# Two sets of weight sums at other places in VectorE's order, in the seven-product part of a feed-forward layer

## The chip, the cores and the metric

The kernel runs on one core of one Trainium2 chip. The metric is the device time of one execution in microseconds (us); the time of a kernel is the median of its runs.

## The reference

A trunk of two layers (`DEPTH = 2`) on 256 tokens of width 1024, in float32. Each layer is a feed-forward block, a mixing block (a state-space group beside a gated group), and a second feed-forward block; a final RMSNorm ends it. The change lies in the second feed-forward block:

```python
def swiglu(h, w_in, w_out):
    gu = h @ w_in
    g, u = gu[..., :D_FF], gu[..., D_FF:]
    return (jax.nn.silu(g) * u) @ w_out

for l in range(DEPTH):
    x = x + 0.5 * swiglu(rmsnorm(x, norm_ffn1[l]), ffn1_w_in[l], ffn1_w_out[l])
    ...
    x = x + 0.5 * swiglu(rmsnorm(x, norm_ffn2[l]), ffn2_w_in[l], ffn2_w_out[l])
```

`D_FF` is 2816, which is 22 tiles of 128 (`FT`) or 11 blocks of 256 (`UB`).

## The kernel before

Every product is made from numbers split in two parts: `hi`, a copy in the matmul's own format (float32r), and `lo`, the rest. A product is then three matmuls (`three`, L501 to L503: hi x hi, hi x lo, lo x hi). ScalarE makes `hi` (`ACTIVATE` with Copy), VectorE makes `lo` (a subtraction).

**Halves and slots.** Weights come in through three `raw` buffers of 1 MB, issued by SyncE, and are split into a ring of four halves (`RING = 4`), `w_hi` and `w_lo`. A half is 128 rows x 1024. The halves of a feed-forward block are numbered by h from its start: h = 0 to 43 are the up projection (4 per block of 256 hidden columns, 11 blocks), h = 44 to 65 the 22 rows tiles of the down projection. The same number orders ScalarE's and VectorE's work by hand: each walks over h, and tables say which further work stands at which h. TensorE consumes a half and counts `half_done`; ScalarE may split half n only after half n - 4 is consumed.

**Seven products.** In ffn2, the second feed-forward block, 12 of the 22 row tiles of the down projection are taken in pairs, as six slots (`SEVEN = (3, ..., 8)`, h = 50 to 61), numbered i = 0 to 5 below. A slot's 2x2 product of blocks is done with seven block products in place of eight (`seven_rows`). For this, sums of the hidden values (`sums_a`, then `hs_hi`, `hs_lo`) and sums of the weights are needed. The weights are loaded a second time into an `area` (two in `sums_b`, two more over the memory of `x_hi` and `x_lo`, which is free when the up projection has ended). `sums_make` builds four sums in an area with four VectorE operations (L1334, L1336, L1338, L1340), each of which waits for the one before. `sums_split` makes `s_hi` on ScalarE (L994) and `s_lo` on VectorE (L1348). There are two `s_hi`/`s_lo` buffers; ScalarE writes one only after TensorE has finished the slot two before (`seven_done`). The plain weights of such a slot are split as one wide operation of 1536 columns at its even h (L1007 on ScalarE, L1319 on VectorE).

**TensorE's waits.** At the first slot, and at each after it, TensorE waits for all the hidden values and for the wide split; it then does three products (nine matmuls) with plain weights, waits for the slot's `s_lo`, and does four more (twelve matmuls):

```python
pe.wait_ge(hlo_done, UB * f + UB)
pe.wait_ge(salo_done, l * N7 + i + 1)
...
pe.wait_ge(lo_done, half(l, h) + 2)
...
pe.wait_ge(slo_done, m + 1)
```

**VectorE's order.** `ffn` walks over h, and inside one h the order is fixed:

```python
split(l, UPS[j] + h)
if j:
    sums_split(l, h)
    sums_make(l, h)
if j and h - 1 in HIDDEN_AT and HIDDEN_AT.index(h - 1) in SEVEN:
    sums_lo(l, HIDDEN_AT.index(h - 1))
if h in HIDDEN_AT:
    hidden_lo(l, j, HIDDEN_AT.index(h))
```

`HIDDEN_AT` places the hidden blocks; its last three entries, for blocks 8, 9 and 10, are 4 UB + 5, 4 UB + 6 and 4 UB + 7, with 4 UB = 44. `hidden_lo` (L1445) writes `h_lo` and counts `hlo_done`. `SUMS_AT`, `SPLIT_AT` and `LOAD_AT` place the sums, the splits of the sums and the loads of the areas, one entry for each slot i.

Of the kernel before, what the change touches and what calls it, by code (L numbers as in the profile page):

```python
# [19 lines left out]
UB = FF // 256  # L20
# [53 lines left out]

AREA = (0, 1, 0, 1, 2, 3)
LOAD_AT = (26, 28, 36, 38, 4 * UB + 8, 4 * UB + 10)
SUMS_AT = (25, 29, 36, 41, 4 * UB + 9, 4 * UB + 12)
SPLIT_AT = (28, 31, 4 * UB + 11, 4 * UB + 13, 4 * UB + 15, 4 * UB + 17)
FOLD_AT = 4 * UB + 2 * SEVEN[-1] + 5

# [58 lines left out]
def build(nc, a, out):  # L139
    stack = ExitStack()  # L140
    with stack:
# [1164 lines left out]
        def _(dve):  # L1306
# [20 lines left out]
            def sums_make(l, h):  # L1327

                for i in range(N7):
                    if SUMS_AT[i] == h:  # L1330
                        m = l * N7 + i
# [598 lines left out]
```

## Time and profile before

| | |
|---|---|
| median of 3 runs | 907.9 us (907.88 to 907.93) |
| the profiled execution | 907.8 us |
| its span, first to last instruction | 906.1 us |
| TensorE matmul busy | 897.4 us (99%) |
| VectorE busy | 620.3 us (68%) |
| ScalarE busy | 507.4 us (56%) |
| GpSimd busy | 371.8 us (41%) |
| mean DMA rate | 193 GB/s |

Engines are named PE (TensorE matmul), PEld (TensorE weight load), DVE (VectorE), ACT (ScalarE), POOL (GpSimd) and SP (SyncE). A line of the timeline has the start in us, the length in us, the engine, the line of the kernel, the operation, out<-in, and the count of merged instructions. In brackets stands how long the engine was idle before it and what released it. Matmuls are pipelined: the length of one reaches over the start of the next, so their pace is read from their starts. Layer 0's ffn2 has its down projection from about 391 us, layer 1's from about 837 us.

### The profile page before, as it was taken

The page shows a single profiled execution, that of the slowest core. Times are in us where ns is not written, and L with a number is a line of the kernel's source. Part 1 is how long each engine was busy: PE and PEld are TensorE (multiplying, and loading weights), DVE is VectorE, ACT ScalarE, POOL GpSimd, SP SyncE. Part 2 cuts the span into 40 slices and gives each one's busy share as a digit, 9 for nine tenths or more (in the row PEclk, how much of TensorE's full clock was granted, in tenths as well). Part 3 has the DMA queues.
Part 4 walks back from the last instruction along what each step waited for, and adds up shares of the span by engine and source line. Part 5 has one row for each costly group of instructions (what it writes and reads, how often), then busy time and mean ns, then how long its engine had stood idle before and what let it go on. Part 6 is the DMA issues. An engine that isn't in the chain of part 4 may idle for free.

```text
span 906.1 us, 12882 instructions
## 1 busy us (share of the span) xinstructions
PE 897.4 (99%) x4935; PEld 743.1 (82%) x4935; DVE 620.3 (68%) x729; ACT 507.4 (56%) x741; POOL 371.8 (41%) x574
## 2 busy tenths in 40 slices
PE   9999999999999999999999999999999999999997
PEld 7888888888878888887888888888888888888886
DVE  5555665458976578868965656653888855789597
ACT  6544454458766456646464445445677654656474
POOL 3488999894510000000055889988734100000000
PEclk9999999999999999999999999999999999999999
DMA  9786555544256677684559665555344476785751
GB/s 281 196 271 188 186 184 180 175 160 142 94 194 200 196 251 230 229 283 159 186 175 246 186 188 186 186 186 186 120 160 143 139 221 196 263 270 188 267 175 46
DMA packets 138381, 174.60 MB, mean 193 GB/s; under 512 B 18760, under 2 KB 110032, under 8 KB 138320
## 3 DMA queue, kind: packets, MB, share of 16 engines
q1 hardware_dynamic: 138032, 173.24, 59.7%
q8 instruction: 39, 0.64, 0.3%
q10 hardware_dynamic: 288, 0.53, 0.2%
q14 instruction: 22, 0.18, 0.1%
HBM read 172.70 MB, written 1.05 MB: 192 GB/s over the span
## 4 chain that ended last, share of the span: by engine, by line
PE 95%; DVE 3%; issue 1%; DMA 1%; ACT 1%; SPq 0%; ACTq 0%; DVEq 0%
PE bank L501 29%; PE bank L503 29%; PE bank L502 29%; PE bank L606 2%; DVE w_lo L1319 1%; PE bank L511 1%; PE bank L833 1%; DVE s_lo L1348 1%; DMA raw<-in_ffn_w_in 1%; PE bank L861 0%; PE bank L851 0%; PE bank L874 0%; PE bank L716 0%; ACT w_hi L1007 0%; PE bank L937 0%
## 5 line engine op out<-in xcount | busy, mean ns | idle before, releaser
L1324 DVE TENSOR_TENSOR w_lo<-raw,w_hi 128x1024 fp32r<-128x1024 f32 x278 | 351.0, 1271 | 214.4 <-ACT w_hi L1016 214.2
L1016 ACT ACTIVATE w_hi<-raw 128x1024 fp32r<-128x1024 f32 x278 | 292.7, 1061 | 242.0 <-PE bank L503 223.2
L501 PE MATMUL bank<-w_hi,x_hi 128*128 128x512 f32 x856 | 336.5, 393 | 0.0
L503 PE MATMUL bank<-w_hi,x_lo 128*128 128x512 f32 x856 | 333.5, 390 | 0.0
L502 PE MATMUL bank<-w_lo,x_hi 128*128 128x512 f32 x856 | 333.2, 389 | 0.0
L501 PEld LDWEIGHTS bank<-w_hi,x_hi 128*128 128x128 f32 x856 | 160.7, 188 | 35.2 <-issue 2.5
L503 PEld LDWEIGHTS bank<-w_hi,x_lo 128*128 128x128 f32 x856 | 160.7, 188 | 33.7
L502 PEld LDWEIGHTS bank<-w_lo,x_hi 128*128 128x128 f32 x856 | 160.8, 188 | 32.3
L1664 POOL TENSOR_TENSOR rstd_c<-ms_c,neg_half 128x2 f32<-128x2 f32 (+1 forms) x7 | 7.7, 1106 | 394.9 <-DVE ms_c L1367 394.9
L501 PE MATMUL bank<-w_hi,h_hi 128*128 128x512 f32 (+1 forms) x283 | 111.0, 392 | 0.0
L503 PE MATMUL bank<-w_hi,h_lo 128*128 128x512 f32 (+1 forms) x283 | 109.7, 387 | 0.0
L502 PE MATMUL bank<-w_lo,h_hi 128*128 128x512 f32 (+1 forms) x283 | 109.6, 387 | 0.0
L1079 ACT ACTIVATE sil<-bank,rstd_c 128x256 f32<-128x256 f32 x88 | 36.8, 470 | 53.2 <-PE bank L503 53.1
L501 PEld LDWEIGHTS bank<-w_hi,h_hi 128*128 128x128 f32 x283 | 53.1, 188 | 11.4 <-DVE h_lo L1445 0.6
L503 PEld LDWEIGHTS bank<-w_hi,h_lo 128*128 128x128 f32 x283 | 53.1, 188 | 11.0
L502 PEld LDWEIGHTS bank<-w_lo,h_hi 128*128 128x128 f32 x283 | 53.2, 188 | 10.4
L1655 POOL TENSOR_TENSOR sc<-sc 128x16 f32<-128x16 f32 (+1 forms) x154 | 55.2, 358 | 12.3
L1428 DVE SCALAR_TENSOR_TENSOR hid<-bank,rstd_c,sil 128x256 f32<-128x256 f32 x88 | 38.5, 479 | 24.4 <-ACT sil L1079 24.4
L1655 POOL TENSOR_TENSOR pt<-sc,bp 128x256 f32<-128x256 f32 x56 | 52.6, 940 | 4.4
L1658 POOL TENSOR_SCALAR sc<-sc 128x16 f32<-128x16 f32 (+1 forms) x90 | 38.7, 430 | 7.7
L1655 POOL TENSOR_TENSOR bp<-pt 128x256 f32<-128x256 f32 x32 | 36.3, 1133 | 2.5
L1319 DVE TENSOR_TENSOR w_lo<-raw,w_hi 128x1536 fp32r<-128x1536 f32 x12 | 21.0, 1753 | 12.9 <-ACT w_hi L1007 12.9
(231 smaller groups left out, 886.9 us busy)
## 6 DMA issues: line engine op xcount, KB each, us to landing
raw<-in_ffn_w_in SPq DMA_DIRECT2D x172, 512.0 KB
raw<-in_ffn_w_out SPq DMA_DIRECT2D x32, 1024.0 KB
raw<-in_mix_w_in SPq DMA_DIRECT2D x12, 1024.0 KB
raw<-in_mix_w_out SPq DMA_DIRECT2D x8, 1024.0 KB
sums_b<-in_ffn_w_out SPq DMA_DIRECT2D x16, 512.0 KB, 6.9
raw<-in_ffn_w_out SPq DMA_DIRECT2D x12, 512.0 KB
area<-in_ffn_w_out SPq DMA_DIRECT2D x8, 512.0 KB, 6.4
raw<-in_ffn_w_out SPq DMA_DIRECT2D x12, 256.0 KB
```

What stands on the lines that cost most here:

```text
L501: mm(o, hi_a, hi_b, start=first, stop=False)
L502: mm(o, hi_a, lo_b, start=False, stop=False)
L503: return mm(o, lo_a, hi_b, start=False, stop=last)
L511: ins = nc.tensor.transpose(turned(pair, j)[:, h * P:h * P + P], x[:, h, k * P:k * P + P], ident[:, :])
L606: ins = nc.tensor.transpose(hidden_bank(l, j, b)[:, c:c + P], hid[:, b % 4, h, ft * P:ft * P + P], ident[:, :])
L1016: A(w_hi[:, n % RING, :], raw[:, s, (n % 2) * 1024:(n % 2) * 1024 + 1024], ACT.Copy).then_inc(hi_done, 1)
L1079: A(sil[:, b % 2, t, :], bank[2 * pair + t][:, 0:256], ACT.Silu, scale=rstd_c[:, t:t + 1]).then_inc(sil_done, 1)
L1319: TT(w_lo[:, n % RING:n % RING + 2, :].rearrange("p s m -> p (s m)")[:, 0:1536], raw[:, s, 0:1536], w_hi[:, n % RING:n % RING + 2, :].rear ...
L1324: TT(w_lo[:, n % RING, :], raw[:, s, (n % 2) * 1024:(n % 2) * 1024 + 1024], w_hi[:, n % RING, :].bitcast(F32), ALU.subtract).then_inc(lo_d ...
L1428: STT(hid[:, b % 4, t, :], bank[2 * pair + t][:, 256:512], rstd_c[:, t:t + 1], sil[:, b % 2, t, :], ALU.mult, ALU.mult).then_inc(hid_done, 1)
L1655: link(nc.gpsimd.tensor_tensor(o, x0, x1, op))
L1658: link(nc.gpsimd.tensor_scalar(o, x0, s1, s2, op0, op1))
```

## The change

Two entries of the table `SUMS_AT` change. The four sums of slot i=4 stand at h = 51 in place of 53, and those of slot i=5 at h = 58 in place of 56. Loads, splits and everything on the other engines keep their places.

```diff
 AREA = (0, 1, 0, 1, 2, 3)
 LOAD_AT = (26, 28, 36, 38, 4 * UB + 8, 4 * UB + 10)
-SUMS_AT = (25, 29, 36, 41, 4 * UB + 9, 4 * UB + 12)
+SUMS_AT = (25, 29, 36, 41, 4 * UB + 7, 4 * UB + 14)
 SPLIT_AT = (28, 31, 4 * UB + 11, 4 * UB + 13, 4 * UB + 15, 4 * UB + 17)
```

## Rows read from the trace of the kernel before

**Rows 1.** The page: span, busy time by engine, chain that ended last.
```profile
span 906.1 us, 12882 instructions
...
PE 897.4 (99%) x4935; PEld 743.1 (82%) x4935; DVE 620.3 (68%) x729; ACT 507.4 (56%) x741; POOL 371.8 (41%) x574
...
PE 95%; DVE 3%; issue 1%; DMA 1%; ACT 1%; SPq 0%; ACTq 0%; DVEq 0%
```

**Rows 2.** The chain in order of time, layer 0: start, length, what.
```profile
413.64 1.50 ACT w_hi L1007
...
428.01 2.29 DVE s_lo L1348
```

**Rows 3.** TensorE's timeline, layer 0, slots i=0 and i=3.
```profile
413.13 0.39 PE L503 MATMUL bank<-w_hi,h_lo 128*128 128x512 f32 x1
413.40 0.50 PE L501 MATMUL bank<-w_hi,h_hi 128*128 128x512 f32 x1
...
418.30 0.39 PE L501 MATMUL bank<-w_hi,h_hi 128*128 128x512 f32 x1
...
429.64 0.39 PE L503 MATMUL bank<-w_hi,h_lo 128*128 128x512 f32 x1
430.35 0.50 PE L501 MATMUL bank<-s_hi,hs_hi 128*128 128x512 f32 x1 [0.32 <-DVE s_lo L1348]
...
433.20 0.39 PE L501 MATMUL bank<-w_hi,h_hi 128*128 128x512 f32 x1
```

**Rows 4.** TensorE's timeline, layer 1, the same two places.
```profile
859.71 0.50 PE L501 MATMUL bank<-w_hi,h_hi 128*128 128x512 f32 x1
...
876.65 0.50 PE L501 MATMUL bank<-s_hi,hs_hi 128*128 128x512 f32 x1 [0.33 <-DVE s_lo L1348]
```

**Rows 5.** VectorE's timeline, layer 0, from h = 50 to h = 54.
```profile
409.79 1.76 DVE L1319 TENSOR_TENSOR w_lo<-raw,w_hi 128x1536 fp32r<-128x1536 f32 x1 [4.58 <-ACT w_hi L1007]
411.47 0.68 DVE L1452 TENSOR_TENSOR hs_lo<-sc,hs_hi_last 128x512 fp32r<-128x512 f32 x1
412.07 1.28 DVE L1445 TENSOR_TENSOR h_lo<-bank,h_hi 128x512 fp32r<-128x512 f32 x2
415.23 1.76 DVE L1319 TENSOR_TENSOR w_lo<-raw,w_hi 128x1536 fp32r<-128x1536 f32 x1 [1.88 <-ACT w_hi L1007]
416.90 0.69 DVE L1334 TENSOR_TENSOR area<-area 128x512 f32<-128x512 f32 x1
...
419.69 1.75 DVE L1319 TENSOR_TENSOR w_lo<-raw,w_hi 128x1536 fp32r<-128x1536 f32 x1
```

**Rows 6.** TensorE's weight loads, timeline, ahead of slot i=0.
```profile
413.40 0.19 PEld L501 LDWEIGHTS bank<-w_hi,h_hi 128*128 128x128 f32 x1 [0.31 <-DVE h_lo L1445]
```

**Rows 7.** Windows: us, PE, PEld, DVE, ACT, POOL busy, clock, DMA share, GB/s.
```profile
404.00:408.00 4.00, 4.00 (x19) 3.28 (x19) 1.18 (x3) 0.00 (x0) 0.00 (x0) 1.00 0.97 339
408.00:412.00 4.00, 4.00 (x20) 3.30 (x18) 2.21 (x2) 2.98 (x4) 0.00 (x0) 1.00 0.06 23
```

**Rows 8.** VectorE's timeline, layer 0, from h = 57 to h = 59.
```profile
428.01 2.28 DVE L1348 TENSOR_TENSOR s_lo<-sums_b,s_hi 128x2048 fp32r<-128x2048 f32 x1
430.21 1.75 DVE L1319 TENSOR_TENSOR w_lo<-raw,w_hi 128x1536 fp32r<-128x1536 f32 x1
431.88 2.28 DVE L1348 TENSOR_TENSOR s_lo<-area,s_hi 128x2048 fp32r<-128x2048 f32 x1
```

**Rows 9.** ScalarE's timeline, layer 0, `s_hi` of slots i=2 and i=3.
```profile
418.56 1.92 ACT L994 ACTIVATE s_hi<-sums_b 128x2048 fp32r<-128x2048 f32 x1 [1.21 <-PE bank L503]
...
423.32 1.93 ACT L994 ACTIVATE s_hi<-sums_b 128x2048 fp32r<-128x2048 f32 x1 [1.20 <-PE bank L503]
```

**Rows 10.** Windows at the end of the span, columns as in rows 7.
```profile
900.00:901.00 1.00, 0.17 (x2) 0.00 (x0) 0.80 (x3) 0.84 (x4) 0.83 (x1) 1.00 0.74 168
...
903.00:903.50 0.50, 0.00 (x0) 0.00 (x0) 0.00 (x0) 0.00 (x0) 0.00 (x0) 0.95 0.62 131
903.50:904.00 0.50, 0.00 (x0) 0.00 (x0) 0.00 (x0) 0.00 (x0) 0.00 (x0) 0.50 0.86 180
```

## The prediction

> **What bounds the kernel now.** I read the page first. TensorE is busy for 897.4 of 906.1 us and makes 95% of the chain that ended last; VectorE has 3% of it [rows 1]. So the time is TensorE's queue plus its few gaps, and a change in VectorE's order counts only where it opens or closes a gap on TensorE. Next I read the chain in order of time around the edited step, the second half of ffn2. From 413.64 to 430.30 us in layer 0 it leaves TensorE and runs through ScalarE and VectorE up to a split of sums, `s_lo` L1348 [rows 2]. VectorE is the limit of that stretch, and the gap that it leaves on TensorE is all that a better order can win.
>
> I took the size of that gap from TensorE's timeline. Matmuls of a seven-product step start every 0.227 us: from 413.40 to 418.30 are 21 of them and a start-up (below), and without a wait a step is 21 x 0.227 = 4.76 us. Step i=3 shows the gap: from the matmul at 429.64 to the first of step i=4 at 433.20 are 13 starts, which would be 2.95 us; it took 3.56. The gap is 0.61 us per layer, released by `s_lo` L1348 [rows 3]. Layer 1 has the same wait at 876.65 [rows 4]. Two gaps of 0.61 are 1.2 us, 0.13% of the time, the most that the change can win. Two runs of this kernel can be told apart from about 0.2% (1.8 us) on, so that gain alone would not show.
>
> **Where the moved work lands.** A slot's sums are four VectorE operations of 128x512, L1334 to L1340. In the kernel before, those of slot i=4 start at 416.90 and the next operation starts at 419.69: 2.79 us [rows 5]. No operation is added or removed, and no DMA, wait or other queue moves; only VectorE's order changes. What counts is what stands behind the 2.79 us in each new place.
>
> *Slot i=4, from h = 53 to h = 51.* In `ffn` on VectorE the body of h runs `sums_make` before `hidden_lo`. HIDDEN_AT has 4 UB + 6 = 50 for block 9 and 4 UB + 7 = 51 for block 10. So the order in the stretch from 409.79 was: wide split of h = 50, `hs_lo`, `h_lo` of block 9, `h_lo` of block 10 [rows 5]. Now the four sums stand between the two `h_lo`. The two took 1.28 us together from 412.07, and one alone takes 0.68, as `hs_lo` of the same size does, so the second started at 412.67 and ended at 413.35.
>
> Who waits for that second `h_lo`? TensorE does: ahead of the first seven-product step it waits for `hlo_done` of all 11 blocks (UB * f + UB). The last ordinary matmul started at 413.13 and the next could start at 413.36. It started at 413.40, 0.05 us after `h_lo` ended [rows 3], and the weight load in front of it has an idle time of 0.31 us with DVE `h_lo` L1445 as its releaser [rows 6]. There is no slack to speak of: VectorE arrives 0.01 us before TensorE is ready to go on. That is the observation on which the forecast rests.
>
> The new times: sums from 412.67 to 415.46, `h_lo` of block 10 to 416.14, TensorE starts at 416.19 in place of 413.40. **The new stall costs 2.79 us per layer.** Nothing moves it earlier. The wide split of h = 50 starts at 409.79 after 4.58 us in which VectorE waited for ScalarE [rows 5], and from there VectorE works without a pause to the `h_lo`. The sums' input is there: the DMA engines were still at 97% until 408 us and at 6% from 408 to 412, so the transfers of the two areas, issued ahead of that, have landed [rows 7]. No cost for a wait on the transfer, then; if it were late, VectorE would wait at the sums and all of that would be added.
>
> Can TensorE make the 2.79 us up later? No: it has no idle time to give but the gap of 0.61 us, and every later step is queued behind.
>
> *Slot i=5, from h = 56 to h = 58.* These sums stood ahead of `s_lo` of slot i=3, which TensorE was waiting for at 430.35 [rows 3, 8]. Now they stand behind it. In addition TensorE is 2.79 us later. ScalarE's `s_hi` of slot 3 follows TensorE's step i=1 and moves with it from 423.32 to 426.11, ending at 428.04 [rows 9]. VectorE is free by then: `s_hi` of slot 2, which ran from 418.56 for 1.92 us [rows 9], moves by 2.79 too and ends at 423.27; `s_lo` takes 2.20 and a wide split 1.67 after it [rows 8], which makes 427.2. So `s_lo` of slot 3 runs from 428.08 to 430.36, and TensorE needs it at 429.87 + 2.79 = 432.66. **The old gap goes: -0.61 us per layer.**
>
> What is late next? Behind it stand the wide split of h = 58, the sums of slot 5 and `s_lo` of slot 4. From one start to the next, `s_lo` takes 2.20 us and a wide split 1.67 [rows 8]. So the split starts at 430.28, the sums at 431.95, `s_lo` of slot 4 at 434.74, and it ends at 437.02. TensorE starts step i=4 at 433.20 - 0.61 + 2.79 = 435.38 and needs `s_lo` after nine matmuls, at 437.42. The margin is 0.40 us: thin, but it holds by these rows. `s_lo` of slot 5 ends at 434.74 + 2.20 + 1.67 + 2.28 = 440.89 and is needed at 442.18; a margin of 1.3 us. After that come plain splits, where VectorE is ahead.
>
> **The sum.** Per layer +2.79 - 0.61 = +2.18 us, in two layers +4.36 us. Layer 1 runs the same way: from TensorE's start at step i=0 to its wait in step i=3 are 876.65 - 859.71 = 16.94 us there [rows 4] and 430.35 - 413.40 = 16.95 us in layer 0 [rows 3]. The profiled execution took 907.8 us (span 906.1 and 1.7 around it), and the median of the runs is 907.9. Both give the same shift: 907.9 + 4.4 = 912.3 us, +0.48%.
>
> **A page against a row.** TensorE will stand still for about 2.7 us in each layer, longer than anywhere in the span now. At the end of the span its last matmul starts before 900.2; the granted clock is still 1.00 in the stretch to 903, 0.95 in the one to 903.5 and 0.50 (the lower level, 1.2 GHz) from then on [rows 10]. So it fell some 3.3 us after the work ended, and 2.7 us of idle time is shorter than that. The Trainium skill ("TensorE: Matmul & The Clock Gate", "Why this matters for your kernels") warns of idle gaps between bursts of matmuls, because the engine goes back to its lower level after them. By the row the sum stays 912.3; by the rule, if this gap counted, it would be the 915.6 of the second rival.
>
> **Rivals.**
> 1. *The new wait isn't exposed; only the old gap closes.* If TensorE had slack at the first seven-product step, the sums of slot 4 would hide under its rows and the 1.2 us would be won: 906.7 us, not slower. For it: VectorE was idle for 4.58 us just before, so on a mean there is room. Against it: that room lies ahead of the wide split, not between the two `h_lo`, and TensorE's weight load already waits for `h_lo` [rows 6]. It would take more than 2 us of slack for this side to win; the rows show 0.01. Chance 0.07.
> 2. *The clock falls in the stall.* If TensorE came back at 1.2 GHz and stayed there for as long as it takes to fall, 3.3 us, half of that would be lost: 1.65 us per layer, 3.3 in all, 915.6 us. For it: the instant of the fall is known here only once. Against it: 2.7 is under 3.3, and in the 0.61 us gap the clock didn't move. Chance 0.05.
> 3. *The margin of 0.40 us at step i=4 doesn't hold.* The gap then comes back there: up to the 0.61 us of the old one, 1.2 us in all, 913.5 us. Speaking for it: VectorE works without a pause from 428.08 on, and a delay of each of its four steps by 0.1 us uses the margin up. Against: the same operations took the same time to within 0.01 us in all of this stretch. Chance 0.08.
>
> **How the numbers follow.** My forecast has 0.80: 912.3 us, its own range 911.7 to 913.0 (a tenth of a microsecond on each of the eight edges, and the start-up after a longer wait, of which the trace has only short examples). The range is 911.3 to 913.9: the forecast and rival 3, with a little on both sides for a stall a few tenths smaller or larger than the sum says. Rivals 1 and 2 lie outside. Slower by over 0.2%: forecast, rivals 2 and 3, 0.93. Rival 1 is -0.13%, so most of its 0.07 falls within 0.2%: same 0.05, faster 0.02.
>
> **What the profile after would show.** In TensorE's timeline an idle time of about 2.7 us ahead of the first matmul of step i=0 near 416.2 us, released by DVE `h_lo` L1445, and the same in layer 1 near 864.7. In VectorE's timeline four `area` operations between two single `h_lo`. No wait for `s_lo` L1348 in the middle of step i=3. Granted clock 1.00 right after the stall. `s_lo` of slot 4 ends within half a microsecond of TensorE's need. The prediction is wrong if TensorE's start at step i=0 doesn't move, if the chain keeps `s_lo` of slot 3, or if the clock reads less than 1.00 after 416 us.

## The result and the profile after

The changed kernel takes 915.45 us (median of 6 runs, 914.48 to 915.94) against 908.03 us before: a ratio of 1.008, 95% interval 1.0067 to 1.0093. It is 7.4 us slower. The sign and the place are as forecast, but the time lies 1.5 us above the range and the loss is 1.7 times the 4.4 us of the sum. It comes out where the second rival put it, at 915.6 us.

The profiled execution of the changed kernel took 915.6 us with a span of 913.9. TensorE's timeline around the first seven-product step of layer 0, which answers to [rows 3]:

```profile
413.33 0.39 PE L503 MATMUL bank<-w_hi,h_lo 128*128 128x512 f32 x1
416.39 0.50 PE L501 MATMUL bank<-w_hi,h_hi 128*128 128x512 f32 x1 [2.67 <-DVE h_lo L1445]
416.73 0.39 PE L502 MATMUL bank<-w_lo,h_hi 128*128 128x512 f32 x1
416.96 0.50 PE L503 MATMUL bank<-w_hi,h_lo 128*128 128x512 f32 x1
417.25 0.63 PE L501 MATMUL bank<-w_hi,hs_hi 128*128 128x512 f32 x1
417.68 0.63 PE L502 MATMUL bank<-w_lo,hs_hi 128*128 128x512 f32 x1
...
420.24 0.52 PE L502 MATMUL bank<-s_lo,hs_hi 128*128 128x512 f32 x1
420.60 0.39 PE L503 MATMUL bank<-s_hi,hs_lo 128*128 128x512 f32 x1
...
422.91 0.39 PE L501 MATMUL bank<-w_hi,h_hi 128*128 128x512 f32 x1
```

Two things are to be seen. TensorE stands idle for 2.67 us, released by `h_lo`. And after the restart the next starts come after 0.34, 0.23 and 0.29 us, then every 0.43 us in place of 0.227, until about 420.5 us. The windows of the same stretch tell why (columns as in [rows 7]; the clock is the third figure from the right):

```profile
415.00:416.00 1.00, 0.00 (x0) 0.00 (x0) 0.97 (x3) 0.33 (x1) 0.00 (x0) 1.00 0.19 72
416.00:417.00 1.00, 0.61 (x3) 0.53 (x4) 1.00 (x2) 0.00 (x0) 0.00 (x0) 1.00 0.00 0
417.00:418.00 1.00, 1.00 (x4) 0.80 (x3) 1.00 (x1) 0.00 (x0) 0.00 (x0) 0.55 0.00 0
418.00:419.00 1.00, 1.00 (x4) 0.72 (x4) 0.00 (x0) 0.00 (x0) 0.00 (x0) 0.50 0.00 0
419.00:420.00 1.00, 1.00 (x4) 0.82 (x3) 0.00 (x0) 0.00 (x0) 0.00 (x0) 0.50 0.97 207
420.00:422.00 2.00, 2.00 (x10) 1.61 (x9) 0.28 (x1) 1.49 (x1) 0.00 (x0) 0.87 0.76 289
422.00:424.00 2.00, 2.00 (x10) 1.68 (x9) 1.48 (x1) 0.83 (x1) 0.00 (x0) 1.00 0.00 1
```

The granted clock is 1.00 through the whole idle time. It falls to 0.50 at about 417.1 us, when TensorE has been at work again for 0.7 us, and comes back at about 420.5. Layer 1 does the same:

```profile
863.44 0.39 PE L503 MATMUL bank<-w_hi,h_lo 128*128 128x512 f32 x1
866.49 0.50 PE L501 MATMUL bank<-w_hi,h_hi 128*128 128x512 f32 x1 [2.66 <-DVE h_lo L1445]
...
873.02 0.39 PE L501 MATMUL bank<-w_hi,h_hi 128*128 128x512 f32 x1
```

VectorE's timeline shows the moved sums between the two `h_lo`, as answer to [rows 5], and slots 3 and 4 behind, as answer to [rows 8]:

```profile
410.00 1.76 DVE L1319 TENSOR_TENSOR w_lo<-raw,w_hi 128x1536 fp32r<-128x1536 f32 x1 [4.58 <-ACT w_hi L1007]
411.67 0.68 DVE L1452 TENSOR_TENSOR hs_lo<-sc,hs_hi_last 128x512 fp32r<-128x512 f32 x1
412.27 0.68 DVE L1445 TENSOR_TENSOR h_lo<-bank,h_hi 128x512 fp32r<-128x512 f32 x1
412.88 0.68 DVE L1334 TENSOR_TENSOR area<-area 128x512 f32<-128x512 f32 x1
...
415.65 0.68 DVE L1445 TENSOR_TENSOR h_lo<-bank,h_hi 128x512 fp32r<-128x512 f32 x1
416.25 1.75 DVE L1319 TENSOR_TENSOR w_lo<-raw,w_hi 128x1536 fp32r<-128x1536 f32 x1
...
429.88 2.29 DVE L1348 TENSOR_TENSOR s_lo<-sums_b,s_hi 128x2048 fp32r<-128x2048 f32 x1 [0.80 <-ACT s_hi L994]
...
436.54 2.28 DVE L1348 TENSOR_TENSOR s_lo<-area,s_hi 128x2048 fp32r<-128x2048 f32 x1
```

From start to start the sums still take 415.65 - 412.88 = 2.77 us. The old gap at step i=3 is gone from the list of TensorE's waits in the changed kernel.

**The loss by rows.** In layer 0 the step starts 416.39 - 413.33 = 3.06 us after the matmul before it, and 0.27 us after it in [rows 3]: 2.79 us lost, the term of the sum. The step then takes 422.91 - 416.39 = 6.52 us, against 4.90 in [rows 3]: 1.62 us more. Layer 1 has 3.05 us ahead of the step, of which 0.28 were there before (859.71 - 859.43), and 6.53 us for the step. With the old gap gone, a layer loses 2.79 + 1.62 - 0.61 = 3.80 us, the two 7.6; the spans differ by 7.8, and 0.2 of this was there before the first edited stretch (413.33 against 413.13).

### The profile page after: what moved, and what is told of

Read it like the earlier page. It is cut to its first block, busy times and chain, and to the rows that moved or that the text cites. A ratio compares the mean times of both kernels' runs of the same rounds, so it can differ in the third digit from the quotient of the medians.

```text
span 913.9 us, 12882 instructions
## 1 busy us (share of the span) xinstructions
PE 901.0 (99%) x4935; PEld 746.5 (82%) x4935; DVE 620.7 (68%) x729; ACT 507.4 (56%) x741; POOL 370.7 (41%) x574
## 4 chain that ended last, share of the span: by engine, by line
PE 97%; DVE 1%; ACT 0%; issue 0%; POOL 0%; ACTq 0%; POOLq 0%; DVEq 0%
PE bank L501 30%; PE bank L503 29%; PE bank L502 29%; PE bank L606 2%; PE bank L511 1%; PE bank L833 1%; PE bank L861 0%; PE bank L851 0%; PE bank L966 0%; PE bank L874 0%; DVE w_lo L1319 0%; PE bank L716 0%; ACT w_hi L1007 0%; PE bank L937 0%; PE bank L539 0%; DVE h_lo L1445 0%
## 5 line engine op out<-in xcount | busy, mean ns | idle before, releaser
L1655 POOL TENSOR_TENSOR sc<-sc 128x16 f32<-128x16 f32 (+1 forms) x154 | 59.1, 384 | 12.3
L1658 POOL TENSOR_SCALAR sc<-sc 128x16 f32<-128x16 f32 (+1 forms) x90 | 34.2, 380 | 7.7
```

The lines of the kernel that those rows point to most:

```text
L1655: link(nc.gpsimd.tensor_tensor(o, x0, x1, op))
L1658: link(nc.gpsimd.tensor_scalar(o, x0, s1, s2, op0, op1))
```

## Experiments

The medians are those of 5 or 11 runs. The times of the kernel before beside them were 908.12 us (slot 5 alone, slot 4 alone, no sum ahead, 24 transposes) and 908.26 us (12 transposes and one, two and three sums ahead).

### Slot 5 alone

```diff
-SUMS_AT = (25, 29, 36, 41, 4 * UB + 9, 4 * UB + 12)
+SUMS_AT = (25, 29, 36, 41, 4 * UB + 9, 4 * UB + 14)
```

> Only slot i=5 moves (h = 56 to 58); slot i=4 stays at h = 53. Theory: this half closes the old gap of 0.61 us per layer at step i=3 and opens none, since s_lo of slot 4 would end near 434.2 us and TensorE needs it near 434.6. Expected 906.7 us (907.9 - 1.2), clock 1.00 throughout. Rival (the move of slot 5 itself costs something at step i=4): 908 us or more, with a wait for s_lo L1348 one step later.

Measured: 906.84 us, ratio 0.9983 (0.9974 to 0.9992). This half gains 1.3 us, the 1.2 of the sum. TensorE's timeline at step i=3 runs at full pace over the place of the old gap:

```profile
430.20 0.39 PE L503 MATMUL bank<-w_hi,h_lo 128*128 128x512 f32 x1
430.43 0.39 PE L501 MATMUL bank<-s_hi,hs_hi 128*128 128x512 f32 x1
430.66 0.39 PE L502 MATMUL bank<-s_lo,hs_hi 128*128 128x512 f32 x1
```

The start behind the wait comes 0.23 us after the one ahead of it, where [rows 3] have 0.71. The rival falls: no wait for `s_lo` appears one step later.

### Slot 4 alone

```diff
-SUMS_AT = (25, 29, 36, 41, 4 * UB + 9, 4 * UB + 12)
+SUMS_AT = (25, 29, 36, 41, 4 * UB + 7, 4 * UB + 12)
```

> Only slot i=4 moves (h = 53 to 51); slot i=5 stays at h = 56. Theory: the whole loss comes from this half, the stall of 2.7 us before the first seven-product step and the fall of the clock behind it, and the delay of TensorE also covers the old wait for s_lo of slot 3. Expected 915.4 us, like the changed kernel, clock 0.995. Rival (the 0.61 us per layer were won back by the move of slot 5): 916.6 us, with a wait for s_lo L1348 in step i=3.

Measured: 915.62 us, ratio 1.0078 (1.0065 to 1.0091), the time of the changed kernel. The row of TensorE's waits that names slot work (total us, times, longest us):

```profile
PE bank L501 <- DVE h_lo L1445: 5.3, 2, 2.7
```

That is two waits of 2.7 us for `h_lo`, and none for `s_lo`. So the whole loss is slot 4's, and in its company slot 5's move gains nothing: TensorE is so late that the old wait vanishes by itself.

The trace of this kernel also shows when a fall may come. TensorE's timeline and the windows, layer 0:

```profile
413.62 0.39 PE L503 MATMUL bank<-w_hi,h_lo 128*128 128x512 f32 x1
416.67 0.79 PE L501 MATMUL bank<-w_hi,h_hi 128*128 128x512 f32 x1 [2.66 <-DVE h_lo L1445]
```

```profile
416.00:416.25 0.25, 0.00 (x0) 0.00 (x0) 0.25 (x2) 0.00 (x0) 0.00 (x0) 1.00 0.00 0
416.25:416.50 0.25, 0.00 (x0) 0.00 (x0) 0.25 (x1) 0.00 (x0) 0.00 (x0) 0.58 0.00 0
```

The idle time begins at 414.01 us and the clock falls at about 416.3, some 2.3 us later and 0.4 us before TensorE starts again. In layer 1 it falls at about 866.85 us, 3.0 us after the idle time began. The time from the start of the idle time to the fall isn't a constant. Part of the fall of layer 0 costs nothing, since it lies in the idle time: the step takes 423.00 - 416.67 = 6.33 us there, 0.19 less than in the changed kernel.

### The sums of slot 4 behind the last `h_lo`

The changed kernel, with its new table, but at h = 51 the four sums stand at the end of the body. `sums_make` is written as a loop for this, with the same four operations in the same order; its third argument says which of them it does:

```diff
-                        sums_make(l, h)
+                        sums_make(l, h, range(0) if h == HIDDEN_AT[-1] else range(4))
...
                     if h in HIDDEN_AT:
                         hidden_lo(l, j, HIDDEN_AT.index(h))
+                    if j and h == HIDDEN_AT[-1]:
+                        sums_make(l, h, range(0, 4))
```

> The changed kernel with the four sums of slot i=4 at the end of the body of h = 51, behind h_lo of block 10 in place of ahead of it. Theory (TensorE loses only because the sums stand ahead of that h_lo; behind it VectorE has an idle 1.9 us before the next wide split, and 0.5 us of margin at step i=1): no stall, clock 1.00, old gap gone: 906.7 us. Rival (sums this early cost something whatever stands behind them, through the wide split of h = 52 or the ring): 909 us or more.

Measured: 906.86 us, ratio 0.9986 (0.9977 to 0.9995). One operation of 0.6 us changes sides with the four sums, and 8.6 us come back. VectorE's timeline (a loop makes the four sums one line here):

```profile
412.38 1.28 DVE L1444 TENSOR_TENSOR h_lo<-bank,h_hi 128x512 fp32r<-128x512 f32 x2
413.58 2.86 DVE L1339 TENSOR_TENSOR area<-area 128x512 f32<-128x512 f32 x4
416.36 3.42 DVE L1319 TENSOR_TENSOR w_lo<-raw,w_hi 128x1536 fp32r<-128x1536 f32 x2
```

The sums fill the 1.88 us in which VectorE waited for ScalarE before [rows 5]; the wide splits behind are later for it, but TensorE's list of waits has none for `w_lo`. The sums may be that early; they may only not stand ahead of that `h_lo`.

### TensorE kept at work during its wait, for 2.8 us and for 1.5 us

The changed kernel, with 24 or 12 transposes of the identity in each layer that add nothing to the result (the next product that is written to their bank starts it anew):

```diff
                             i = SEVEN.index(k // 2)
+                            if i == 0:
+                                for _ in range(24):
+                                    nc.tensor.transpose(bank[2 * c0 + 1][:, 0:P], ident[:, :], ident[:, :])
                             pe.wait_ge(hlo_done, UB * f + UB)
```

> The changed kernel, and TensorE does 24 transposes of the identity into an unused bank (about 0.109 us each, 2.6 us) in each layer ahead of its wait for h_lo, so that it is delayed as before but not idle. Theory A (the excess over the predicted 912.3 us is the clock that falls after the idle time): clock 1.00, 912.3 us. Theory B (the excess is something else in the longer stall, such as later weights or a slower restart): 915.4 us, clock figures notwithstanding.

> The changed kernel with 12 transposes (1.3 us) ahead of TensorE's wait for h_lo: the same delay of 2.79 us, but only 1.4 us of it idle. Theory A (it is the length of idle time that makes the clock fall, not the delay): clock 1.00 and 913.0 us, as with 24 transposes. Theory B (the delay matters, or any stall here): 915.4 us.

Measured: 913.00 us with 24 (ratio 1.0053, 1.004 to 1.0065) and 912.59 us with 12 (1.0047, 1.0034 to 1.006). TensorE's timeline with 24:

```profile
414.26 2.78 PE L788 MATMUL bank<-ident 128*128 128x128 f32 x24
417.08 0.50 PE L501 MATMUL bank<-w_hi,h_hi 128*128 128x512 f32 x1
417.42 0.39 PE L502 MATMUL bank<-w_lo,h_hi 128*128 128x512 f32 x1
417.65 0.40 PE L503 MATMUL bank<-w_hi,h_lo 128*128 128x512 f32 x1
417.89 0.39 PE L501 MATMUL bank<-w_hi,hs_hi 128*128 128x512 f32 x1
```

and with 12:

```profile
414.48 1.47 PE L788 MATMUL bank<-ident 128*128 128x128 f32 x12
417.30 0.50 PE L501 MATMUL bank<-w_hi,h_hi 128*128 128x512 f32 x1 [1.35 <-DVE h_lo L1448]
417.64 0.40 PE L502 MATMUL bank<-w_lo,h_hi 128*128 128x512 f32 x1
```

The windows of the same stretch, with 24 and with 12:

```profile
412.00:422.00 10.00, 9.96 (x57) 8.44 (x56) 7.46 (x10) 3.06 (x3) 0.00 (x0) 1.00 0.46 149
```

```profile
417.30:422.00 4.70, 4.70 (x20) 3.86 (x21) 2.23 (x2) 1.49 (x1) 0.00 (x0) 1.00 0.43 130
```

The step starts as late as in the changed kernel, but the matmuls behind it keep their pace of 0.23 us and the clock stays at 1.00. More work on TensorE makes the kernel 2.5 to 2.9 us faster than the changed one. Against their own runs of before they cost 4.9 and 4.3 us, where the sum without a clock term says 4.4. So the delay is priced rightly, and the excess goes with the idle time and not with the delay; an effect of late weights would have stayed. That it is the clock, and not another slowness after a long idle time, is read from the changed kernel: the starts come every 0.43 us just where its windows read 0.50.

### One, two and three of the four sums ahead of the last `h_lo`

As the third experiment, with `range(n)` ahead and `range(n, 4)` behind.

> One of the four sums stands ahead of the last h_lo. Delay 0.6 to 0.7 us, idle time about 0.5 us, no more than the old gap at step i=3, behind which the clock stayed: 907.9 us by both theories (the new gap is as large as the old one), clock 1.00.

> Two of the four sums stand ahead of the last h_lo. Delay 1.33 us, idle time about 1.2 us. Theory A: no fall, 907.9 + 2 x (1.33 - 0.61) = 909.3 us. Theory B: 912.3 us.

> Three of the four sums of slot i=4 stand ahead of the last h_lo at h = 51, the fourth behind it. TensorE's delay is 3 x 0.72 less the overlap, 2.06 us; its idle time about 1.9 us. Without a fall of the clock 907.9 + 2 x (2.06 - 0.61) = 910.8 us; with a fall in both layers (1.5 us each, as the changed kernel shows) 913.8 us. Theory A (the fall needs an idle time near that of the changed kernel, 2.7 us): 910.8. Theory B (any stall at this place makes it fall): 913.8.

| sums ahead of `h_lo` | TensorE idle before step i=0, us | expected without a fall, us | measured, us (lowest to highest) | ratio, interval |
|---|---|---|---|---|
| 0 | none | 906.7 | 906.86 (906.24 to 907.29) | 0.9986 (0.9977 to 0.9995) |
| 1 | 0.5 | 907.9 | 908.16 (907.66 to 909.04) | 0.9999 (0.999 to 1.0008) |
| 2 | 1.2 | 909.3 | 909.50 (909.17 to 909.96) | 1.0014 (1.0005 to 1.0023) |
| 3 | 1.9 | 910.8 | 911.72 (910.6 to 912.7) | 1.0037 (1.0024 to 1.0049) |
| 4 (the changed kernel) | 2.7 | 912.3 | 915.45 (914.48 to 915.94) | 1.008 (1.0067 to 1.0093) |

The expected times start from 907.9 us. Up to two sums the price follows the delay alone. With three, both theories are half right: the two layers of the profiled execution go different ways after the same idle time. TensorE's timeline of that kernel, layer 0 and then layer 1, and a window of layer 1:

```profile
415.28 0.50 PE L501 MATMUL bank<-w_hi,h_hi 128*128 128x512 f32 x1 [1.94 <-DVE h_lo L1444]
...
420.20 0.39 PE L501 MATMUL bank<-w_hi,h_hi 128*128 128x512 f32 x1
...
862.99 0.50 PE L501 MATMUL bank<-w_hi,h_hi 128*128 128x512 f32 x1 [1.94 <-DVE h_lo L1444]
...
864.26 0.53 PE L503 MATMUL bank<-w_hi,hs_lo 128*128 128x512 f32 x1
864.58 0.63 PE L501 MATMUL bank<-w_hi,h_hi 128*128 128x512 f32 x1
...
869.54 0.39 PE L501 MATMUL bank<-w_hi,h_hi 128*128 128x512 f32 x1
```

```profile
864.00:866.00 2.00, 2.00 (x7) 1.55 (x6) 1.21 (x1) 0.00 (x0) 0.00 (x0) 0.59 0.00 0
```

Step i=0 takes 4.92 us in layer 0 and 6.55 in layer 1, where the clock fell about 1.4 us after the restart. One fall costs 1.63 us, read from one execution with everything else alike. Whether it comes after 1.9 us of idle time is not the same from one place to the next.

The other runs have no profile, but each has a mean granted clock. It is 0.995 in the two profiled executions with two falls, 0.997 in the one with one fall, and 0.998 to 1.000 in every run of the kernels whose profile shows no fall before the end of the span. Read by this scale, which is an inference, the five runs with three sums ahead had no fall in two (910.60 and 911.23 us; clock 0.998 and 0.999) and one in the other three (911.72, 912.15 and 912.70 us; 0.996, 0.997 and 0.997; the 0.996 fits least well). And 2.7 us of idle time doesn't bring a fall each time either: of the 11 runs of the changed kernel and of slot 4 alone, three read 0.997 (914.48, 914.22 and 914.39 us) and eight 0.995 (915.01 to 916.06 us).

## Why the prediction failed, by its steps

- *What bounds the kernel; a gain of at most 1.2 us.* Right. Slot 5 alone gave 1.3.
- *Slot 4 lands ahead of the `h_lo` that TensorE waits for, 2.79 us per layer.* Right to 0.02 us in both layers (2.79 and 2.77), and shown by moving the sums behind that `h_lo`, which takes all of it away.
- *Slot 5's move closes the old gap, -0.61 us per layer.* Right as a size (slot 5 alone), wrong as a cause inside the whole change: with slot 4 alone the gap is gone too, and the time is the same. Once TensorE is 2.8 us later, `s_lo` of slot 3 is in time in either order. The sum counts the term rightly, as a property of the delay.
- *The margin of 0.40 us at step i=4.* Right: `s_lo` of slot 4 ended at 438.82 us, and the matmul behind TensorE's wait for it started at 439.23, 0.41 us later. Both are 1.8 us later than forecast: ScalarE and VectorE followed TensorE's delay. The third rival didn't happen.
- *"2.7 us of idle time is shorter than that."* **This is the step that failed.** I read from [rows 10] that the clock fell 3.3 us after the last matmul of the span, took this as the idle time which a fall needs, and so put the clock at nothing in the sum. It cost 3.2 us, 1.62 in each layer. The row was one example with nothing behind it. In the changed kernel the idle time was 2.7 us and the fall came 3.4 us (layer 0) and 3.8 us (layer 1) after it began, when the matmuls were running again; with slot 4 alone, layer 0, it came after 2.3 us. At the end of the span, too, the 3.3 us of [rows 10] are only one of several values: by the windows there it is 2.7 us with 12 transposes and 4.2 us with three sums ahead. How much idle time suffices can't be read from how late one fall comes. A clock below 1.00 after 416 us is the sign by which the prediction itself said it would be wrong.
- *The second rival* had the mechanism and nearly the size: 1.65 us per fall by its estimate, 1.62 in the trace; what was wrong was its chance of 0.05. The size was in part luck. The rival let TensorE come back at the lower level and stay there for the 3.3 us that the fall had taken. In the changed kernel TensorE came back at 1.00, fell after 0.7 and 1.2 us of work, and then stayed low for 3.4 us. That the two lengths should be alike had no reason in the rows.
- *The rule of the Trainium skill* ("TensorE: Matmul & The Clock Gate", "Why this matters for your kernels"), which warns of idle gaps between bursts of matmuls. The trace bears out the warning but not its size: the gap from which on the Trainium skill warns is longer than the 2.7 us that brought a fall in both layers here, so by its letter this gap was safe, and the prediction cited the warning without that length. 1.2 us brought none. The one row that I let decide wasn't a measurement of a gap between matmuls.

What stays open: at which idle time a fall becomes certain, and what makes places with the same idle time differ. The few runs with 1.9 us can't tell how often it falls.

## What to carry to other kernels

Before an operation is moved earlier in an in-order engine, look at what follows it in the new place and who waits for that, not at how idle the engine is around it; here the 4.6 us of idle time stood on the wrong side of the one operation with no slack. On TensorE, price a new stall as its length and, where it is as long as those that brought a fall here (1.9 us in one of two profiled places, 2.7 in four of four), a clock fall of 1.6 us behind it; the fall isn't certain, so the range should hold the time with it and without it. Where a stall can't be avoided, a few matmuls to an unused bank ahead of the wait fit into it and keep the clock: 12 transposes per layer, with 1.35 us of idle time left behind them, gave 2.9 us back here.

The version to keep is slot 5's move alone, 906.84 us; with the sums of slot 4 behind `h_lo` it is the same, 906.86. Both beat the kernel before by 0.14 to 0.17%; their intervals end at 0.9992 and 0.9995, just short of no gain.

## What the runs showed of the hardware

- The granted clock of TensorE fell to 0.50 after TensorE had been at work again for 0.7 and 1.2 us (changed kernel, 2.7 us of idle time) and for 1.4 us (three sums ahead, 1.94 us); with slot 4 alone it fell 0.4 us before the work began again in layer 0 and 0.3 us after it in layer 1. It stayed low for 3.4 us, in the changed kernel from about 417.1 to 420.5 us.
- Matmuls of 512 columns started every 0.43 us in that stretch and every 0.227 us outside.
- Idle times of 1.2 to 1.4 us, four of them in two profiles (two sums ahead, 12 transposes), brought no fall; of 1.94 us one in two; of 2.7 us four in four (the changed kernel and slot 4 alone). These are single profiled executions; by their mean clocks, three of the 11 runs with 2.7 us had one fall in place of two.
